# Up units of the FFN's later steps as seven quarter products, on an input that is normed once

## The reference, cut to what matters

```
h = rmsnorm(x) * g                          # x: 512 x 1024
gate = h @ w_in[:, :2816]; up = h @ w_in[:, 2816:]
y = (silu(gate) * up) @ w_down              # 2816 x 1024
```

## Time and profile before

| what | value |
|---|---|
| median of 3 runs | 2888.19 us (2884.27 to 2891.73) |
| the profiled execution, its own time | 2888.17 us |
| its span, first to last instruction | 2886.4 us |
| granted TensorE clock, mean | 0.987 of 2.4 GHz |
| VectorE busy | 1854.0 us (64%) |
| ScalarE busy | 1034.9 us (36%) |
| fast steps in the program | 40 (5 FFNs of 8) |

### The profile page before, as it was taken

The page is one execution under the profiler, slowest core; times in us unless marked ns, Lnnn a source line. Parts: engine busy times, 40 slices in busy tenths (PEclk is TensorE's granted clock), DMA queues, the critical chain, the costliest instruction groups (busy, mean ns, idle before and its releaser), DMA issues.

```text
span 2886.4 us, 37744 instructions
## 1 busy us (share of the span) xinstructions
PE 2802.3 (97%) x15194; PEld 2413.3 (84%) x15194; DVE 1854.0 (64%) x2763; ACT 1034.9 (36%) x1445; POOL 62.6 (2%) x22
## 2 busy tenths in 40 slices
PE   7999999999989999899999999999999899899998
PEld 7878789888878988689887888888889788688897
DVE  4555555555667857678574686764867587658574
ACT  4343444443343322433224332322323256423232
POOL 0000011110000000000000000000000000000000
PEclk9999999999999999999999999999999999899999
DMA  7223322323532333223222233231333343123321
GB/s 217 88 77 103 114 74 65 94 91 112 181 116 88 103 102 105 101 88 108 97 95 97 77 113 103 96 109 66 110 103 102 116 160 108 59 77 114 102 96 67
DMA packets 262175, 295.15 MB, mean 102 GB/s; under 512 B 6210, under 2 KB 248018, under 8 KB 259342
## 3 DMA queue, kind: packets, MB, share of 16 engines
q1 hardware_dynamic: 257008, 281.53, 29.6%
q10 hardware_dynamic: 5022, 11.57, 1.1%
HBM read 276.30 MB, written 16.78 MB: 102 GB/s over the span
## 4 chain that ended last, share of the span: by engine, by line
PE 93%; DVE 4%; ACT 2%; issue 1%; DMA 0%; ACTq 0%; SPq 0%; DVEq 0%
PE bank L1369 19%; PE bank L1370 19%; PE bank L1371 19%; PE bank L1788 5%; PE bank L1786 5%; PE bank L1787 5%; PE bank L1619 5%; PE bank L1677 2%; PE bank L1935 1%; PE bank L1667 1%; PE bank L1384 1%; PE bank L1385 1%; PE bank L1386 1%; PE bank L1639 1%; PE bank L1638 1%
## 5 line engine op out<-in xcount | busy, mean ns | idle before, releaser
L1369 PE MATMUL bank<-h_hi,w_hi 128*128 128x512 f32 x1424 | 561.8, 395 | 20.2 <-DVE h_lo L2406 16.7
L1370 PE MATMUL bank<-h_lo,w_hi 128*128 128x512 f32 x1424 | 557.3, 391 | 0.0
L1371 PE MATMUL bank<-h_hi,w_lo 128*128 128x512 f32 x1424 | 556.8, 391 | 0.0
L2028 DVE TENSOR_TENSOR w_lo<-w_raw,w_hi 128x2048 fp32r<-128x2048 f32 (+2 forms) x180 | 398.1, 2213 | 172.0 <-ACT w_hi L807 168.7
L807 ACT ACTIVATE w_hi<-w_raw 128x2048 fp32r<-128x2048 f32 (+2 forms) x174 | 318.4, 1840 | 512.7 <-PE bank L1371 453.2
L1369 PE MATMUL bank<-hid_hi,w_hi 128*128 128x512 f32 x880 | 343.8, 391 | 1.5 <-DVE w_lo L2028 1.5
L1371 PE MATMUL bank<-hid_hi,w_lo 128*128 128x512 f32 x880 | 342.4, 389 | 0.0
L1370 PE MATMUL bank<-hid_lo,w_hi 128*128 128x512 f32 x880 | 342.4, 389 | 0.0
L1369 PEld LDWEIGHTS bank<-h_hi,w_hi 128*128 128x128 f32 x1424 | 269.1, 189 | 79.2 <-issue 22.5
L1371 PEld LDWEIGHTS bank<-h_hi,w_lo 128*128 128x128 f32 x1424 | 268.9, 189 | 56.6
L1370 PEld LDWEIGHTS bank<-h_lo,w_hi 128*128 128x128 f32 x1424 | 269.2, 189 | 55.4 <-issue 1.2
(11 more groups left out here) (425 smaller groups left out, 5050.4 us busy)
## 6 DMA issues: line engine op xcount, KB each, us to landing
w_raw<-in_ffn_w_in_dram SPq DMA_DIRECT2D x88, 1024.0 KB, 5.0
w_raw<-in_ffn_w_out_dram SPq DMA_DIRECT2D x32, 1024.0 KB, 5.1
w_raw<-in_w_in_dram SPq DMA_DIRECT2D x28, 1024.0 KB, 5.1
w_raw<-in_w_ffn_in_dram SPq DMA_DIRECT2D x22, 1024.0 KB, 5.0
w_raw<-in_ffn_w_out_dram SPq DMA_DIRECT2D x16, 768.0 KB, 4.3
w_raw<-in_conv_w_pw_dram SPq DMA_DIRECT2D x12, 1024.0 KB, 6.8
phase_taps<-in_conv_dw_phases_dram SPq DMA_DIRECT2D x10, 1152.0 KB, 8.0
w_raw<-in_w_ffn_down_dram SPq DMA_DIRECT2D x8, 1024.0 KB, 5.2
```

The source lines that it names most:

```text
L1369: nc.tensor.matmul(bank[b][:, 0:n], wh, xh, start=first, stop=False)
L1370: nc.tensor.matmul(bank[b][:, 0:n], wh, xl, start=False, stop=False)
L1371: ins = nc.tensor.matmul(bank[b][:, 0:n], wl, xh, start=False, stop=last)
L2028: v.tensor_tensor(w_lo[slot][:, 0:n], raw[s][:, 0:n], w_hi[slot][:, 0:n].bitcast(F32), ALU.subtract).then_inc(w_lo_ready, 1)
```

## The change

- An up unit of steps 3 to 10 becomes seven quarter products as well, with tables of its own (`up_quarters_hi`, `up_quarters_lo`) and PSUM banks 2, 3, 6 and 7. All 40 of them are concerned.
- x is normed once. In steps 1 and 2 VectorE writes x times gain times `rb` to `x_normed` (`normed`, eight operations on 512 tokens). In down column 1 of the first part it makes the four sums of quarters from that (`x_sums_of_all`, four operations of 1024), ScalarE writes the high parts over `h_hi` (two operations of 2048), and VectorE writes the low parts over `h_lo` (`normed_low`, two of 2048). The 16 small sums of before and ScalarE's `x_first_half_gained` go.
- Fast steps no longer multiply by `rb`.
- The high part of the hidden tile moves from VectorE to ScalarE (`hidden_high`). The multiplication and the split of a step's hidden tiles move behind the start of the next step (`multiply`, `hidden_low`).
- The sums of an up unit's weight quarters are made in the step before, or in down column 4. One buffer, `weight_sums`, serves all units in turn.

The diff, cut to its core (the helper `seven_products` on TensorE is the seven-product list of before with the unit as an argument):

```diff
-QUADS = {gate_unit(_f, _i) for _f in range(5) for _i in range(3, UP_STEPS)}
-IN_THIRD = {_u + 1 for _u in QUADS} | {down_unit(_f, _p, 3) for _f in range(5) for _p in range(2)}
+GATE_QUADS = {gate_unit(_f, _i) for _f in range(5) for _i in range(3, UP_STEPS)}
+UP_QUADS = {gate_unit(_f, _i) + 1 for _f in range(5) for _i in UP_FAST}
+QUADS = GATE_QUADS | UP_QUADS
+QUAD_AT = {_u: _n for _n, _u in enumerate(sorted(QUADS))}
...
 for _u in range(N_UNITS):
     WIDTH.append(UNIT)
-    if _u in QUADS:
+    if _u in UP_QUADS:
+        _s = None
+        NEED.append(_last.get(2, -1) + 1)
+        _last[2] = _u
+    elif _u in GATE_QUADS:
         _s = None
         NEED.append(max(_last[0], _last[1]) + 1)
...
-Q_PLACE = ((0, 0), (1, 0), (0, 1), (5, 0), (5, 1), (1, 1), (4, 0))
+Q_PLACE = (((0, 0), (1, 0), (0, 1), (5, 0), (5, 1), (1, 1), (4, 0)), ((2, 0), (3, 0), (2, 1), (7, 0), (7, 1), (3, 1), (6, 0)))
...
+        q_hi = [at("gate_quarters_hi", [P, 7, KT // 2, P], W0 + 16 * KB + Q_AT, F32R),
+                at("up_quarters_hi", [P, 7, KT // 2, P], AR + 32 * KB + Q_AT, F32R)]
+        q_lo = [at("gate_quarters_lo", [P, 7, KT // 2, P], W0 + 32 * KB + Q_AT, F32R),
+                at("up_quarters_lo", [P, 7, KT // 2, P], AR + 110 * KB + Q_AT, F32R)]
+        up_sum = at("up_sums", [P, KT, T], AR + 46 * KB + 256)
+        up_kept = at("up_products_kept", [P, KT, T], AR + 16 * KB)
+        x_unit = at("x_normed", [P, KT, T], AR + 62 * KB + 512)
...
+                    act.wait_ge(w_summed, W_SUMMED + 3 * QUAD_AT[u] + 3)
+                    nc.scalar.activation(q_hi[u in UP_QUADS][:, 3:7, :, :], w_sum[:, :, :, :], ACT.Copy).then_inc(w_hi_ready, 1)
+                def keep_first(u, dst):
+                    act.wait_ge(qp_made, MADE + 6 * QUAD_AT[u] + 1)
+                    b, half = Q_PLACE[u in UP_QUADS][0]
+                    nc.scalar.activation(dst, bank[b][:, QT * half:QT * (half + 1)], ACT.Copy).then_inc(copied, 1)
+                def hidden_high(i):
+                    for m, t in enumerate((1, 0)):
+                        act.wait_ge(hid_made, HID_MADE + hid_count(f, i) + m + 1)
+                        nc.scalar.activation(hid[0][:, hid_tile(i) + t, :], tg[t][:, :], ACT.Copy).then_inc(hid_high, 1)
...
-                    high(u + 1)
...
+                    u = gate_unit(f, i)
+                    if u + 1 in QUADS:
+                        quarters_high(u + 1)
+                    else:
+                        high(u + 1)
+                    keep_first(u, kept[:, :])
+                    if u + 1 in QUADS:
+                        sums_high(u + 1)
+                    if i - 1 not in (2, 6):
+                        hidden_high(i - 1)
...
                         quarters_high(u + 2)
-                    silu(2 * UP_STEPS * f + 2 * i, (1, 0))
...
                         high(u + 2)
+                    if u + 1 in QUADS:
+                        keep_first(u + 1, up_kept[:, hid_tile(i), 0:QT])
+                    if u + 2 in QUADS:
+                        sums_high(u + 2)
+                    silu(2 * UP_STEPS * f + 2 * i, (1, 0))
...
                 def down_part(p):
                     for c in range(4):
                         u = down_unit(f, p, c)
+                        if p > 0 and c == 0:
+                            hidden_high(PARTS[p][-1])
                         if c < 3:
                             high(u + 1)
                         else:
                             quarters_high(u + 1)
...
+                            sums_high(u + 1)
                         if p == 0 and c == 0:
...
+                            act.wait_ge(x_summed, X_SUMMED + 10 * f + 4)
+                            act.wait_ge(w_used, gate_unit(f, 2) + 2)
+                            for half in range(2):
+                                tiles = slice(4 * half, 4 * half + 4)
+                                nc.scalar.activation(h_hi[:, tiles, :], x_unit[:, tiles, :], ACT.Copy).then_inc(x_act, 1)
                         if p == 0 and c == 1:
...
+                            act.wait_ge(x_summed, X_SUMMED + 10 * f + 6)
                             for m in (1, 2, 0, 3):
                                 nc.scalar.activation(x_sum_hi[:, m, :, :], x_sum[:, m, :, :], ACT.Copy).then_inc(x_act, 1)
...
+                    quarter_product(u, 3, 6, x_quarter(1, 1)).then_inc(w_used, 1)
                 def fast_step(i):
...
+                    u, n = gate_unit(f, i), 2 * i + 2 * UP_STEPS * f
                     pe.wait_ge(w_lo_ready, u + 1)
                     pe.wait_ge(g_scaled, n)
...
+                    seven_products(u, i)
                     pe.wait_ge(w_lo_ready, u + 2)
                     pe.wait_ge(up_read, n)
...
+                    if u + 1 in QUADS:
+                        seven_products(u + 1, i)
+                    else:
+                        products(SLOT[u + 1], KT, UC, (h_hi, h_lo), (2, 3))
...
+                    if p > 0 and c == 1:
+                        pe.wait_ge(up_read, 2 * UP_STEPS * f + 2 * PARTS[p][-1] + 2)
                     if p == 0 and c < 2:
                         pe.wait_ge(up_read, 2 * UP_STEPS * f + 2)
...
+                    for m, t in enumerate((0, 1)):
...
+                def normed(j):
+                    name, r = GAIN_OF[f]
+                    link(v.scalar_tensor_tensor(x_unit[:, j, :], X[:, j, :], col(name, j, r), rb[:, :], ALU.mult, ALU.mult))
                 def up(i):
...
+                        for j in range(4):
+                            normed(4 * (i - 1) + j)
...
-                def weight_sums(u, s):
+                def weight_sums(u):
+                    n = W_SUMMED + 3 * QUAD_AT[u]
+                    dve.wait_ge(w_lo_ready, u)
                     dve.wait_ge(w_landed[u % 2], 16 * (u // 2 + 1))
-                    a11, a12, a21, a22 = (quarter(u % 2, n, k) for n in range(2) for k in range(2))
+                    a11, a12, a21, a22 = (quarter(u % 2, n_, k) for n_ in range(2) for k in range(2))
...
+                    dve.wait_ge(w_summed, n + 1)
...
+                    dve.wait_ge(w_summed, n + 2)
...
+                def low_of_unit(u):
+                    if u in QUADS:
+                        quarters_low(u)
+                        sums_low(u)
+                    else:
+                        weight_low_of(u)
...
+                def combine(u, top, bottom, first, third, read):
+                    n = MADE + 6 * QUAD_AT[u]
+                    b2, b4 = Q_PLACE[u in UP_QUADS][1][0], Q_PLACE[u in UP_QUADS][3][0]
+                    dve.wait_ge(copied, COPIED + QUAD_AT[u] + 1)
+                    dve.wait_ge(qp_made, n + 3)
+                    link(v.tensor_tensor(halves(top), twice(first), halves(bank[b2][:, :]), ALU.add))
+                    dve.wait_ge(qp_made, n + 4)
+                    link(v.tensor_tensor(third, top[:, QT:T], place(u, 7), ALU.add))
+                    dve.wait_ge(qp_made, n + 6)
+                    v.tensor_tensor(halves(bottom), twice(third), halves(bank[b4][:, :]), ALU.add).then_inc(read, 1)
+                    link(v.tensor_tensor(top[:, QT:T], top[:, QT:T], place(u, 5), ALU.add))
+                def combine_last(u, top, read):
+                    dve.wait_ge(w_used, u + 1)
+                    v.tensor_tensor(top[:, QT:T], top[:, QT:T], place(u, 3), ALU.add).then_inc(read, 1)
+                def up_made(i):
+                    return [up_sum[:, hid_tile(i) + t, :] for t in range(2)]
+                def multiply(i):
+                    u, n = gate_unit(f, i) + 1, 2 * i + 2 * UP_STEPS * f
+                    if u in QUADS:
+                        combine_last(u, up_made(i)[0], up_read)
+                        dve.wait_ge(up_read, n + 2)
+                    else:
+                        dve.wait_ge(w_used, u + 1)
+                    for m, t in enumerate((1, 0)):
+                        dve.wait_ge(silu_done, n + m + 1)
+                        if u in QUADS:
+                            v.tensor_tensor(tg[t][:, :], tg[t][:, :], up_made(i)[t], ALU.mult).then_inc(hid_made, 1)
+                        else:
+                            mark(v.tensor_tensor(tg[t][:, :], tg[t][:, :], bank[2 + t][:, :], ALU.mult), hid_made, HID_MADE + hid_count(f, i) + m + 1)
+                            dve.sem_inc(up_read, 1)
+                def hidden_low(i):
+                    n = hid_count(f, i)
+                    dve.wait_ge(hid_made, HID_MADE + n + 2)
+                    dve.wait_ge(hid_high, HID_HIGH + n + 2)
+                    for t in range(2):
+                        j = hid_tile(i) + t
+                        mark(v.tensor_tensor(hid[1][:, j, :], tg[t][:, :], hid[0][:, j, :].bitcast(F32), ALU.subtract),
+                             hid_ready, 2 * i + 2 * UP_STEPS * f + t + 1)
...
+                    u = gate_unit(f, i)
+                    follows = i - 1 not in (2, 6)
+                    if follows:
+                        multiply(i - 1)
+                    low_of_unit(u + 1)
```

(43 more changed lines are left out.)

167 lines of the change are left out of this document (63 added, 104 removed).

## The result

| | before | after |
|---|---|---|
| median | 2889.64 us (16 runs on this chip) | 2894.84 us (16 runs) |
| lowest to highest | 2884.27 to 2896.16 | 2891.23 to 2898.36 |
| profiled execution; its span | 2888.17; 2886.4 | 2891.23; 2889.4 |
| granted TensorE clock, mean | 0.987 | 0.982 |
| VectorE busy | 1854.0 us | 2016.7 us |

The ratio is 1.0019, with an interval of 1.0011 to 1.0027. My forecast was no change that can be told (2887.3, range 2872 to 2904). So some 6 us are mine to find. The profiled execution of after is the fastest of its 16: its granted clock is 0.982, where ten of them have 0.980. So the two profiled executions lie only 3.1 us apart.

What follows compares the result with a forecast made beforehand. TensorE was taken as the bound, busy for 2802.3 of 2886.4 us. The terms summed as 2888.2 - 40.0 + 13.0 + 17.7 + 8.4 = 2887.3 us, range 2872 to 2904.

Steps and rivals of the forecast that it cites:

- Term 1: TensorE, up units of steps 3 to 10: 40 units go from 10.90 to 9.90 us, saving 40.0 us.
- Term 2: VectorE in fast steps: 21.1 us per middle step makes TensorE wait 2.6 us in steps 3 to 6, +13.0 us.
- Term 3: First part's down column 1: VectorE's stall for ScalarE makes TensorE wait 3.55 us before column 3, +17.7 us in five FFNs.
- Term 4: TensorE's clock behind the wait before column 3: half pace costs 1.68 us per FFN, +8.4 us.
- Edits at no cost: Normed x, ScalarE's added work, last hidden tiles and SP's load queue: all were claimed to add no time.
- the last hidden tiles of a part: Behind column 1's start: ready after some 8 us, needed at 8.2; tight, 1 us late would cost 10 us.
- SP's queue: Unit loads wait for a low part up to 5 us later; the sums needing them stand 9.9 us further on.
- The slow rival: VectorE slower in every middle step, 22.0 us instead of 21.1, through the hand-over of sums: 2909 us, chance 15%.

## Why the prediction was wrong

**Term 1 was right.** Four up units save 83.20 - 79.15 = 4.05 us where nothing waits: 40.5 for 40, I had 40.0.

**Term 2 was right in place and a little too large.** I had a middle step at 21.1 us of VectorE and got 20.97, no wait in the third part and waits of some 0.6 us for low parts of sums in the second. Those cost 2.15 us an FFN instead of 2.6, 10.8 for 13.0. With smaller sums they vanished, and with an earlier entry of VectorE TensorE gained some 2 us. My sum took every unit at 9.90 us; that a unit behind a wait can take 9.64 was not in it, and 0.25 us per FFN of the difference are that, at the last unit of the stage.

**Term 3 was right**: 3.58 for 3.55, in all five FFNs, with 0.14 more for the first matmuls behind it. Moving the parts of h a column on took it away.

**Term 4 was right on the mean and wrong as a mechanism.** I charged 1.68 us for each wait; the 30 waits cost 1.70 in the mean, but single ones from nothing to 2.8. I had treated as a property of the idle's length what is in part chance. The row that I took the price from was itself a draw: the same idle of 2.86 or 2.87 us, at the same place in all 13 traces, was followed by a half clock in eight and by none in five, and the changed kernel's profiled execution is one of the five. Terms 3 and 4 together cost 27.7 us in the profiled execution, and I had 26.1.

**What failed is the step "Edits at no cost", at the last hidden tiles of a part.** I made the sum of that chain once, for all parts: 8.0 us against 8.2, tight. It was right in general (7.4 us measured), and its own premise was that the weights of column 2 are there. In the last part of the second FFN they aren't, since SyncE's load of them stands behind the table's. My sentence on SP's queue spoke only of loads that come up to 5 us later in the steps; I had not gone through the queue's list for its other entries. The low part of the hidden tile, which before stood ahead of the late weights, stood behind them after. That is 4.86 us of wait and a half clock, 7.4 us up to the pooling block (56.00 for 48.60 with the load moved), in place of the 1.8 of before: 5.6 more, where my sum had nothing. Moving the load alone took 6.7 us off the median, of which 1.8 were in the kernel before too. The terms came out at -2.0 us in the profiled execution; with these 5.6 they make +3.6, slower than before, and that is inside the interval of the ratio (3.2 to 7.8 us).

The clue was in my own rows. The short wait of the earlier trace rows at 1522.25 is this very late weight low part. I read the row for what the clock does behind it and not for what it says of the place: that the thing which I was about to put the hidden tiles behind was already late there.

The slow rival ended near the truth in sign but not in cause: no middle step of VectorE came near 21.7 us. One thing remains. The profiled execution is 3.0 us of span longer and the medians are 5.2 apart; the difference is within what the half clocks and the first 900 us vary by, and I have not split it further.

## What to carry to other kernels

When an instruction is put behind another one in an engine's list, ask for every place where the list runs, not for the typical one, how late the one ahead can be: go through each DMA queue for an entry that stands ahead of its load, and through the trace of before for any wait on it, however short. A change that saves on the busiest engine and is given back in waits may need only its order mended: the same arithmetic ran 43.5 us faster (medians 2894.84 and 2851.33, on two chips; the first is 5.2 above the kernel before on its chip, the second 38.6 below) once four pieces of work and one load stood a column or a place elsewhere. Fill the idle time of the second engine ahead of a dense stretch, since what decides is how late it enters.
